# One decoder layer on one core: the order of the first down job's products and of three weight splits

## What is computed

```
x = x + 0.5 * SwiGLU_1(RMSNorm(x))              # FFN1: gate, up 1024 -> 2816, down 2816 -> 1024
z = RMSNorm(x) @ w_in ;  x = x + concat(mLSTM(z), GLA(z)) @ w_out
x = x + CrossAttn(RMSNorm(x), memory)           # ends with a product by w_o
x = x + 0.5 * SwiGLU_2(RMSNorm(x))              # FFN2, as FFN1
y = RMSNorm(x)
```

## Time and profile before

| what | value |
|---|---|
| time, median of 3 runs | 1301.96 us (1300.91 to 1302.71) |
| the profiled execution's own time | 1297.84 us |
| its span, first to last instruction | 1296.0 us |
| its mean granted TensorE clock | 0.986 |
| TensorE busy | 1256.2 us (97% of the span) |
| VectorE busy | 932.5 us (72%) |
| ScalarE busy | 617.1 us (48%) |
| GpSimd busy | 196.0 us (15%) |

### The profile page before, as it was taken

The page is one execution under the profiler, slowest core; times in us unless marked ns, Lnnn a source line. Parts: engine busy times, 40 slices in busy tenths (PEclk is TensorE's granted clock), DMA queues, the critical chain, the costliest instruction groups (busy, mean ns, idle before and its releaser), DMA issues.

```text
span 1296.0 us, 25334 instructions
## 1 busy us (share of the span) xinstructions
PE 1256.2 (97%) x10321; PEld 1216.5 (94%) x10321; DVE 932.5 (72%) x1326; ACT 617.1 (48%) x962; POOL 196.0 (15%) x184
## 2 busy tenths in 40 slices
PE   7999999999889999999999999999999999999987
PEld 7999999999889999998888899879999999999987
DVE  5988778888793376667766544535698878888885
ACT  6455455555462233345534622324445545645553
POOL 1112222232100000002111000100012222222210
PEclk9999999999899999998999999999999999999988
DMA  6578887888653223324055673541458888798861
GB/s 203 116 158 171 179 171 154 179 189 169 135 118 102 69 80 82 82 82 131 19 132 171 215 244 112 190 176 55 119 124 179 175 177 167 146 199 174 175 125 69
DMA packets 302324, 185.03 MB, mean 143 GB/s; under 512 B 10582, under 2 KB 290368, under 8 KB 302212
## 3 DMA queue, kind: packets, MB, share of 16 engines
q1 hardware_dynamic: 233072, 125.61, 33.8%
q0 software_dynamic: 68976, 57.68, 25.6%
q10 hardware_dynamic: 164, 0.16, 0.0%
HBM read 175.53 MB, written 7.88 MB: 142 GB/s over the span
## 4 chain that ended last, share of the span: by engine, by line
PE 41%; DVE 6%; issue 1%; ACT 1%; DMA 1%; another core or an unknown queue 0%; POOL 0%; SPq 0%; DVEq 0%; ACTq 0%
PE ps L2194 39%; DVE ring_w L1325 2%; PE ps L2697 1%; DMA slots<-in_ffn_w_up 1%; DVE xs_lo L1346 1%; ACT ring_w L845 0%; PE ps L2802 0%; DVE hs L1466 0%; PE ps L2728 0%; DVE hf L1454 0%; DVE hf L1351 0%; DVE xf L1351 0%; DVE hf L1448 0%; DVE xf L1358 0%
## 5 line engine op out<-in xcount | busy, mean ns | idle before, releaser
L2194 PE MATMUL ps<-xs_hi,ring_w 128*128 128x272 f32 x2016 | 382.7, 289 | 3.1 <-DVE ring_w L1325 3.1
L1325 DVE TENSOR_TENSOR ring_w<-slots,ring_w 128x1024 fp32r<-128x1024 f32 (+3 forms) x262 | 273.8, 1046 | 102.3 <-ACT ring_w L845 101.1
L2194 PEld LDWEIGHTS ps<-xs_hi,ring_w 128*128 128x128 f32 x2016 | 316.6, 188 | 3.8 <-DVE ring_w L1325 3.8
L845 ACT ACTIVATE ring_w<-slots 128x1024 fp32r<-128x1024 f32 (+3 forms) x262 | 238.9, 918 | 156.5 <-DVE slots L1333 83.5
L2194 PE MATMUL ps<-xs_lo,ring_w 128*128 128x272 f32 x1008 | 291.7, 289 | 0.0
L2194 PE MATMUL ps<-hs,ring_w 128*128 128x272 f32 x1848 | 242.6, 292 | 10.4 <-DVE hs L1466 7.6
L2194 PEld LDWEIGHTS ps<-hs,ring_w 128*128 128x128 f32 x1848 | 238.3, 192 | 13.0 <-DVE hs L1466 9.0
L2194 PEld LDWEIGHTS ps<-xs_lo,ring_w 128*128 128x128 f32 x1008 | 189.6, 188 | 0.0
L2194 PE MATMUL ps<-xn_hi,w_hi 128*128 128x272 f32 x736 | 155.9, 292 | 1.9 <-DVE w_lo L1290 1.9
L2194 PE MATMUL ps<-xn_hi,w_lo 128*128 128x272 f32 x736 | 153.9, 289 | 0.0
L2194 PE MATMUL ps<-xn_lo,w_hi 128*128 128x272 f32 x736 | 153.4, 288 | 0.0
(11 more groups left out here) (386 smaller groups left out, 1643.1 us busy)
## 6 DMA issues: line engine op xcount, KB each, us to landing
slots<-in_ffn_w_gate SPq DMA_DIRECT2D x106, 256.0 KB, 3.5
slots<-in_ffn_w_up SPq DMA_DIRECT2D x106, 256.0 KB, 3.5
slots<-in_ffn_w_down SPq DMA_DIRECT2D x80, 256.0 KB, 3.4
raw<-in_w_in SPq DMA_DIRECT2D x30, 512.0 KB, 3.8
slots<-in_ffn_w_gate POOLq DMA_DIRECT2D x36, 256.0 KB, 5.6
slots<-in_ffn_w_up POOLq DMA_DIRECT2D x36, 256.0 KB, 5.5
slots<-in_ffn_w_down POOLq DMA_DIRECT2D x32, 256.0 KB, 5.6
slots<-in_ffn_w_down SPq DMA_DIRECT2D x40, 192.0 KB, 2.7
```

Source lines behind the costliest of these rows:

```text
L845: act.activation(ring_part(g, 0), sources(g), ACT.Copy).then_inc(sem("prod_hi"), 1)
L1325: dve.tensor_tensor(ring_part(g, 1), sources(g), ring_part(g, 0).bitcast(F32), ALU.subtract)\
L2194: return pe.matmul(out, lhsT, rhs, start=start, stop=stop, skip_group_check=onto)
```

## The change

In the down job that follows the last up job, TensorE's order changes. P1 does quads 0 to 2, then P5's quads 0 to 2 follow, then TensorE waits for quad 3's low part one and does P1's quad 3, which ends P1. At P5's own place, behind P6, only its quad 3 is left.

On VectorE three things move. The low split of `U_IN` goes from behind the last `evac_fs` of FFN1 to ahead of it. The low split of FFN2's first group (two products) goes from behind the last `add_block` of w_o to ahead of it and its wait. And `tile_done(J, 1)` runs one step later, at k - 4 instead of k - 3, that is behind `evac_c22` instead of ahead of it.

```diff
                         if p_ == P3:
+                            if n == 0 and k == end - 1:
+                                split(U_IN)
                             evac_fs(J, k)
...
-                    if n == 0 and k == end:
-                        split(U_IN)
...
-                        if after <= k - 1 - 2 * m < end - 1 and kind_at(k - 1 - 2 * m, P3, "down")\
-                           and JOBS[SEQ[k - 1 - 2 * m][0]][1:3] == (n, 2):
-                            tile_done(SEQ[k - 1 - 2 * m][0], m)
+                        if after <= k - 1 - 3 * m < end - 1 and kind_at(k - 1 - 3 * m, P3, "down")\
+                           and JOBS[SEQ[k - 1 - 3 * m][0]][1:3] == (n, 2):
+                            tile_done(SEQ[k - 1 - 3 * m][0], m)
...
                 for k in range(ND):
+                    if k == ND - 1 and u0 == U_XO:
+                        split_lo(G_FIRST[1])
                     dve.wait_ge(pe_unit, u0 + k + 1)
                     add_block(slice(k, k + 1), bufs[k], 1.0)
                     if k == ND - 1 and u0 + k + 2 < N_UNIT:
                         split(u0 + k + 2)
-                    if k == ND - 1 and u0 == U_XO:
-                        split_lo(G_FIRST[1])
...
+            def before_last_quad(i):
+
+                J = SEQ[i][0]
+                n, c = JOBS[J][1:3]
+                k5 = AT[J, P5]
+                pe.wait_ge(sem("prod_lo"), GROUP_OF[i] + 1)
+                pe.wait_ge(sem("x_read"), adders_to(J - 2))
+                h_ready(NF // 2 * n + (CHUNKS[c][0] // 2 + CHUNKS[c][1] - 2), P5)
+                for j in range(CHUNKS[c][1] - 1):
+                    down_triple(i, j, j == 0, False)
+                pe.wait_ge(sem("prod_lo"), GROUP_OF[k5] + 1)
+                pe.wait_ge(sem("fs_read"), nth(J) - 2)
+                for j in range(CHUNKS[c][1] - 1):
+                    down_triple(k5, j, j == 0, False)
+                h_ready(NF // 2 * n + (CHUNKS[c][0] // 2 + CHUNKS[c][1] - 1), 0)
+                down_triple(i, CHUNKS[c][1] - 1, False, True).then_inc(sem("prod_mm"), 1)
...
+                if kind == "down" and J == last_up(n) + 1 and p_ == P1:
+                    before_last_quad(i)
+                    return
                 pe.wait_ge(sem("prod_lo"), GROUP_OF[i] + 1)
+                if kind == "down" and J == last_up(n) + 1 and p_ == P5:
+                    h_ready(NF // 2 * n + (CHUNKS[c][0] // 2 + CHUNKS[c][1] - 1), COMBO[P5])
+                    down_triple(i, nk - 1, False, True).then_inc(sem("prod_mm"), 1)
+                    return
```

More of the change, by code:

```diff
@@ L2310, in plain_product, with down_triple @@
                 ins.then_inc(sem("prod_mm"), 1)
+            def down_triple(i, j, first, last):
+                J, p_ = SEQ[i]
+                m, start = COMBO[p_], p_ in (P1, P5, P2)
+                dst = ps[:, bank_of(J, p_), 0:HT]
+                wh, wl = ring_w[:, ring_slot(i), 0, :], ring_w[:, ring_slot(i), 1, :]
+                cols_ = slice(128 * j, 128 * j + 128)
+                mm(dst, wh[:, cols_], hs[:, j, 0, m, :], start and first, False, not start)
+                mm(dst, wl[:, cols_], hs[:, j, 0, m, :], False, False, not start)
+                return mm(dst, wh[:, cols_], hs[:, j, 1, m, :], False, last, not start)
+            def before_last_quad(i):
[13 more added lines that the diff above has]
+                down_triple(i, CHUNKS[c][1] - 1, False, True).then_inc(sem("prod_mm"), 1)
             def product(i):
```

## The result

The changed kernel takes 1290.15 us (median of 6 runs, 1289.54 to 1293.99) against 1301.28 for the kernel before (6 runs, 1300.57 to 1302.71): ratio 0.9922, 95% interval 0.9911 to 0.9933. The forecast was 1296.0 in 1292.5 to 1299.4, so the direction was right and the size too small. The two medians lie 11.1 us apart; the ratio makes it 10.1. Measured again later (e8), the same kernel gave 0.9945 (0.9932 to 0.9958), 7.1 us, with medians 7.5 apart (1291.38 against 1298.86). The two profiled executions differ by 7.6 (1290.22, span 1288.4, against 1297.84).

The account below looks back on a forecast made before the run. The prediction took TensorE, busy 97% of the span, as the bound, leaving its idle and low-clock time to win. Its terms, 2.6 + 2.2 + 2.1 - 0.9 = 6.0 us off 1301.96, gave 1296.0, range 1292.5 to 1299.4.

Parts of the forecast that it names:

- the job order: Late down jobs of both FFNs: P5's nine matmuls move into TensorE's idle time, 2.6 us won in all.
- the tile order: tile_done(J, 1) behind evac_c22: FFN1's border 0.75 us earlier, FFN2's end 0.9 later, 0.1 us slower in all.
- the two splits: Low splits at FFN1's end and before FFN2 come earlier: 2.1 + 2.1 = 4.2 us faster.
- border 1: FFN1's end into the input projection: the earlier split of U_IN lets TensorE start 2.2 us sooner; bounds 1.2 to 2.9.
- border 2: Passage from w_o to FFN2: the earlier low split removes TensorE's wait, 2.1 us won; bounds 0 to 2.1.
- The border terms: The gains forecast at FFN1's border, 2.2 us, and FFN2's border, 2.1 us.
- Late down jobs: The down job after the last up job, in each FFN: 1.3 us won each, range 0.8 to 2.7.
- Rival B: Clock stays up in both late down jobs, 2.7 us each: 8.8 us less in all, 1293.2; chance 0.17.
- C: FFN2's border gain is given back because VectorE sets the pace: 3.9 us remain, 1298.1; chance 0.20.
- D: Splits do not come early because their high parts are late: 1.7 us remain, 1300.3; chance 0.12.
- End: FFN2's last job: final_gain starts behind evac_c22, so TensorE waits 0.9 us longer; bounds 0 and 0.95.
- E: evac_c22 ahead of tile_done makes VectorE stand for P7's copy: 1.6 us slower, 1303.6; chance 0.04.

Follow-up runs that it names:

- e8: The changed kernel run again with no edit; 1291.38 us, ratio 0.9945 to the kernel before.
- e1: The changed kernel with VectorE's three moves undone, so only TensorE's new order in the late down jobs; 1297.53 us, ratio 0.9977.
- e3: The kernel before with only tile_done(J, 1) moved behind evac_c22; 1299.26 us, ratio 0.9999.
- e2: The kernel before with only the two border splits moved; 1293.13 us, ratio 0.9946.
- e4: The kernel before with 25 unread matmuls in the gap ahead of each late down job's last quad; 1297.9 us, ratio 0.9985.
- e10: The kernel before run again with no edit, to count clock falls at its two borders; 1301.57 us.
- e0: The kernel before run again with no edit, for a second trace; 1299.4 us, ratio 0.9993.
- e11: The kernel before, one more look with no edit, to count clock falls at its two borders; 1299.44 us.
- after: The changed kernel's first profiled execution, no further edit; 1290.22 us against 1297.84 for the kernel before.
- e6: The changed kernel with FFN2's old tile order and 16 unread matmuls ahead of each late job's last quad; 1290.22 us, ratio 0.9928.
- e9: e6 with ScalarE's copy of P1 put ahead of the high split that stood before it; 1290.46 us, ratio 0.9938.
- e5: The kernel before with 15 unread matmuls in each border's gap, ahead of the wait for the low split; 1300.94 us, ratio 1.0008.
- e7: The changed kernel with FFN2's old tile order; 1290.53 us, ratio 0.9927.

## Why the prediction fell short

The forecast took 6.0 us off. The first comparison's interval is 8.7 to 11.6 us; the second's, 5.5 to 8.8, holds the 6.0. By parts, the forecast's steps for the job order (2.6) and the tile order (about nothing) lie inside the intervals of e1 (1.3 to 4.7) and e3; its 4.2 for the two splits lies just below that of e2 (4.3 to 9.6). So what was missing is to be looked for at the borders first.

Counted over all traces whose gap was unfilled, a fall followed the 1.95 us gap at border 1 in 3 of 7 passes (e3, e4, e10) and at border 2 in 3 of 7 (e0, e3, e11). In the kernels without the gap, or with 0.78 to 0.86 us left of it (e2, after, e6 to e9), it followed in 0 of 12. A fall there costs 1.5 us.

**The step that failed** is "Gaps of 1.95 us with full work on both sides left the clock at 1.00". It was read from one execution and taken as a property of the gap. The border terms therefore held the idle time alone and put the clock behind it at nothing; over these traces it costs 6/14 x 1.5 x 2 = 1.3 us on the mean. That the premise fails is shown by the traces. How much it is worth in the timed runs is not shown: e5 filled both gaps, and neither its time nor its clock got better. The Trainium skill, "TensorE: Matmul & The Clock Gate", section "HAM oscillation", puts the fall down to long idle gaps, which is how I reasoned; the traces here disagree, with 0.50 behind gaps of 1.95 us, well short of the 3.36 us of the earlier trace rows.

**Late down jobs:** forecast 1.3 us each, 2.6 in all. The old order's traces (e4 left out) have a mean of 19.43 and 12.16, the new order's unfilled ones (e1, after, e7, e8) 17.62 and 11.31: 1.8 and 0.85, 2.65 in all. The sum is right and its make-up was nearly so. With the gap filled in both orders the clock is out of play: 17.20 and 16.52 in FFN1, 10.30 and 9.59 in FFN2. So the order itself is worth 0.7 (forecast 0.8, with 0.36 for the wait ahead of P7 where FFN1's trace has 0.20), and I take the rest for clock. Rival B's 2.7 was the right size of a job that keeps the clock: 19.43 - 16.50 = 2.9 in FFN1 after. But that is the one of the eight unfilled passes of the new order that kept it; in the other seven it fell to 0.50, so B's condition is rare.

**Border 1:** forecast 2.2, measured 44.95 - 42.46 = 2.5 without a fall; the split alone gives 2.0, the tile order another 0.5. **Border 2:** forecast 2.1, measured 252.9 - 250.63 = 2.3. Nothing came back behind it (200 matmuls that begin some 8 us into FFN2 take 25.06 us in every trace), so C falls. D falls too: the high parts were there, and 0.86 us is left of one gap and nothing of the other. **End:** forecast 0.9 of cost, measured 0.83, the right size. E falls: with the new tile order alone FFN1 got 0.6 us shorter (e3), not longer, and FFN2 lost no more than at its end. (The last 77 matmuls, behind that stage, take 12.8, 14.4 or 15.9 us in traces of the old tile order and of the new.)

**The sum.** 1.8 + 0.85 + 2.5 + 2.3 - 0.8 = 6.6 without falls at the borders, against 6.0, and 1.3 more with them: 7.9 us. That lies inside the second comparison's interval (5.5 to 8.8 us) and 0.8 us under the nearer end of the first's (8.7 to 11.6).

**The base and the range.** I knew that the profiled execution lay 4.1 us under the median and took the same 6.0 us off both. That it had fewer falls to win back than the usual execution is so at the borders: its trace has none, where the seven passes at each have three. Over the whole execution the record does not bear it out: its mean granted clock is 0.986, and the medians over the timed runs of the same kernel in the three later comparisons are 0.986, 0.987 and 0.985. Why it lay 4.1 us under the median is not shown. The range was given "about a microsecond" for this spread, where one unchanged kernel gave 1296.5 to 1303.8.

**Open.** Falls at the borders are counted in 14 passes of profiled executions, not in the timed ones, and e5, which should have shown their mean cost in the time, did not. I have not shown where the 2.2 us between 7.9 and the first comparison's 10.1 come from; they are not there in the second. From the first to the second, the kernel before is 2.4 us faster (1301.28, then 1298.86) and the changed kernel 1.2 slower (1290.15, then 1291.38), whose timed runs had a median granted clock of 0.992 first and 0.988 then. The timed gains of e4 (about half of its trace's) and of e6 over e7 (none) show that one trace for each kernel is too few to sum clock effects from.

## What to carry to other kernels

Before a gap's price is taken from one trace, look at the same gap in several executions: where the granted clock may fall behind it, the price is the idle time plus the share of passes with a fall times its cost. When the profiled execution lies well under the median, the stages that the change touches should be read in a second one too, before a forecast is made for the median. Splits and evacuations that stand behind a wait at a stage border, though their data are long there, are cheap to move: two such splits gave the largest part of this gain.

## What the runs showed of the hardware that was not expected

The clock also falls where TensorE has no gap. In the stage of the decay product, which no kernel here changes, TensorE counts as busy throughout while it does 40 matmuls of small shapes; behind them the clock is at a half in 11 of the 14 traces, for 1.5 us. Timeline, then windows, of the kernel before, and windows of the changed kernel, where it stayed up:

```profile
431.19 2.10 PE L2194 MATMUL ps<-z,a2w 16*128 16x272 f32 x8
433.21 0.93 PE L2194 MATMUL ps<-const 32*32 32x40 f32 x32
```
```profile
432.00:434.00 2.00, 2.00 (x38) 1.51 (x36) 1.24 (x2) 0.41 (x1) 0.00 (x0) 1.00 0.00 0
434.00:436.00 2.00, 2.00 (x14) 1.96 (x11) 0.00 (x0) 0.00 (x0) 0.00 (x0) 0.56 0.46 104
```
```profile
427.00:429.00 2.00, 2.00 (x36) 1.47 (x35) 1.38 (x2) 0.54 (x1) 0.00 (x0) 1.00 0.00 0
429.00:431.00 2.00, 2.00 (x26) 1.96 (x20) 0.00 (x0) 0.00 (x0) 0.00 (x0) 1.00 0.39 86
```

So 1.5 of the 7.6 us between the two profiled executions have nothing to do with the change. Another 1.8 us go the other way: in the product by w_out, which no kernel here changes, TensorE waits 1.55 us for `y_lo` in the kernel before and the clock stays up, and 1.83 us in the changed kernel, where it falls and the same 40 matmuls take 8.6 us instead of 6.8. Timeline and window of the kernel before, then of the changed one:

```profile
651.28 0.36 PE L2194 MATMUL ps<-y_hi,w_hi 128*128 128x272 f32 x1 [1.55 <-DVE y_lo L2018]
652.00:654.00 2.00, 2.00 (x19) 2.00 (x18) 0.46 (x1) 0.00 (x0) 0.00 (x0) 1.00 0.55 207
...
645.02 0.36 PE L2194 MATMUL ps<-y_hi,w_hi 128*128 128x272 f32 x1 [1.83 <-DVE y_lo L2018]
646.00:648.00 2.00, 2.00 (x13) 2.00 (x12) 0.20 (x1) 0.00 (x0) 0.00 (x0) 0.62 0.58 190
```

And matmuls that nobody reads can pay: 25 of them in each late gap of the kernel before kept the clock at 1.00 there and left the kernel 2.0 us faster.

In the middle of FFN2, VectorE waited 2.7 to 5.1 us for a load in all four traces of one chip (e4 to e7) and in e9, and TensorE behind it, for example in e7 (timelines of VectorE and TensorE). In the other nine traces, of old and new kernels alike, VectorE's wait is 0.65 to 1.11 us and TensorE loses at most 0.4. Behind TensorE's wait the clock fell in e4, e5 and e6 (1.95, 4.08 and 2.49 us), but not in e7 (2.29):

```profile
1153.86 0.69 DVE L1333 TENSOR_TENSOR slots<-slots 128x512 f32<-128x512 f32 x1 [3.26 <-DMA slots<-in_ffn_w_up]
...
1156.75 1.36 PE L2194 MATMUL ps<-hs,ring_w 128*128 128x272 f32 x9 [2.29 <-DVE x L1410]
```
